# A decoder trunk's first mixer: q, k and v projected in plain fp32 while the first adaLN products stream, o, x and y from raw weights

## What is computed

```python
c_act = silu(c)
for layer in range(2):
    shift, scale, gate = split(c_act @ ada_w[layer, 0] + ada_b[layer, 0], 3)
    hn = rmsnorm(x, norm_g[layer, 0]) * (1 + scale) + shift
    y = rglru_mlstm_mixer(hn, ...) if layer == 0 else stick_breaking_mixer(hn, ...)
    x = x + gate * y
    shift, scale, gate = split(c_act @ ada_w[layer, 1] + ada_b[layer, 1], 3)
    hn = rmsnorm(x, norm_g[layer, 1]) * (1 + scale) + shift
    x = x + gate * ((silu(hn @ w1) * (hn @ w3)) @ w2)
return rmsnorm(x, final_g)

# mixer of layer 0
xa, ya, q, k, v, o, ig, fg = split(h @ w_in)        # 1024, 1024, 512, 512, 1024, 1024, 4, 4 columns
xa = conv4(xa); out_a = rglru(xa) * gelu(ya)
hb = mlstm_chunkwise(q, k, v, ig, fg)               # 4 heads, running sums of the gates
out_b = norm(hb) * sigmoid(o)
y = concat(out_a, out_b) @ w_out
# mixer of layer 1: q, k, v = h @ w_qkv; 16 heads of stick-breaking attention; o @ w_out
```

## Time and profile before

| | us |
|---|---|
| median of three runs | 2453.87 (2453.47 to 2454.26) |
| profiled execution | 2454.73 |
| its span, first to last instruction | 2453.0 |
| TensorE busy | 2266.0 (92%) |
| VectorE busy | 1887.5 (77%) |
| ScalarE busy | 1028.7 (42%) |
| first product of the output projection of layer 0 | at 406.03 |

### The profile page before, as it was taken

How to read it: one execution, slowest core, us unless ns; L and a number is a source line. 1 busy time by engine, 2 the same in 40 slices (tenths; PEclk the granted TensorE clock), 3 DMA queues, 4 the chain that set the end, 5 groups by cost and what they waited for, 6 DMA issues and landing times.

```text
span 2453.0 us, 36210 instructions
## 1 busy us (share of the span) xinstructions
PE 2266.0 (92%) x12638; PEld 1956.7 (80%) x12638; DVE 1887.5 (77%) x2347; ACT 1028.7 (42%) x1183; POOL 245.9 (10%) x209
## 2 busy tenths in 40 slices
PE   0289998989999999999989999998999999999998
PEld 0277887778888888888878888887888888888887
DVE  7888897988887888778896666678887566666667
ACT  1134456344433443344455455534443344433443
POOL 6100000510000000000240000033000000000014
PEclk9989998999999999999999999999999999999999
DMA  8798775867777776777756655665776555555554
GB/s 345 292 377 312 280 282 210 308 236 282 282 271 286 279 285 270 287 277 289 280 215 272 243 222 219 244 241 212 301 276 255 188 189 188 188 188 188 188 201 159
DMA packets 86186, 619.80 MB, mean 253 GB/s; under 512 B 10216, under 2 KB 10472, under 8 KB 10984
## 3 DMA queue, kind: packets, MB, share of 16 engines
q1 hardware_dynamic: 85248, 617.79, 65.7%
q10 hardware_dynamic: 872, 1.15, 0.1%
HBM read 616.80 MB, written 2.10 MB: 252 GB/s over the span
## 4 chain that ended last, share of the span: by engine, by line
PE 83%; DVE 10%; issue 3%; POOL 2%; ACT 1%; DMA 0%; DVEq 0%; POOLq 0%; ACTq 0%
PE ps L962 49%; PE ps L960 12%; PE ps L965 12%; PE ps L934 4%; DVE adaw L585 3%; DVE wlow L577 3%; PE ps L911 2%; POOL work L381 1%; POOL work L375 1%; PE ps L913 1%; DVE raw L585 1%; ACT whigh L415 1%; DVE work L703 1%; PE ps L1085 1%; DVE hn L709 0%
## 5 line engine op out<-in xcount | busy, mean ns | idle before, releaser
L415 ACT ACTIVATE whigh<-raw 128x1024 fp32r<-128x1024 f32 x784 | 828.0, 1060 | 1182.5 <-PE ps L962 1113.7
L577 DVE TENSOR_TENSOR wlow<-raw,whigh 128x1024 fp32r<-128x1024 f32 x784 | 974.3, 1261 | 391.3 <-ACT whigh L415 382.6
L962 PE MATMUL ps<-hn,whigh 128*128 128x512 f32 x3712 | 1174.6, 397 | 5.1 <-DVE wlow L577 5.1
L962 PE MATMUL ps<-mid,whigh 128*128 128x512 f32 x1856 | 588.0, 397 | 8.5 <-DVE wlow L577 8.5
L962 PEld LDWEIGHTS ps<-hn,whigh 128*128 128x128 f32 x3712 | 569.1, 189 | 7.2 <-issue 6.8
L960 PE MATMUL ps<-hn,wlow 128*128 128x256 f32 x1856 | 517.7, 279 | 0.0
L965 PE MATMUL ps<-hn,wlow 128*128 128x256 f32 x1856 | 515.9, 278 | 0.0
L960 PEld LDWEIGHTS ps<-hn,wlow 128*128 128x128 f32 x1856 | 349.5, 188 | 85.0
L965 PEld LDWEIGHTS ps<-hn,wlow 128*128 128x128 f32 x1856 | 350.3, 189 | 79.6
L585 DVE CUSTOM_DVE_ANT_0 adaw<-adaw,cact 128x2048 f32<-128x2048 f32 x176 | 407.1, 2316 | 5.8 <-DMA adaw<-ada_dram 5.6
L962 PEld LDWEIGHTS ps<-mid,whigh 128*128 128x128 f32 x1856 | 284.9, 189 | 12.2 <-DVE wlow L577 7.6
(11 more groups left out here) (197 smaller groups left out, 1243.6 us busy)
## 6 DMA issues: line engine op xcount, KB each, us to landing
raw<-wts_dram SPq DMA_DIRECT2D x392, 1024.0 KB, 4.8
adaw<-ada_dram SPq DMA_DIRECT2D x176, 1024.0 KB, 6.7
raw<-ada_dram SPq DMA_DIRECT2D x16, 1024.0 KB, 5.6
x<-xT_dram SPq DMA_DIRECT2D x1, 2048.0 KB, 13.9
out_dram<-x SPq DMA_DIRECT2D x4, 512.0 KB, 2.6
cact<-c_row_dram SPq DMA_DIRECT2D x1, 1024.0 KB, 5.1
work<-lru_w_dram ACTq DMA_DIRECT2D x1, 1024.0 KB, 6.6
mod<-ada_b_dram SPq DMA_DIRECT2D x1, 96.0 KB, 4.3
```

The costliest lines, as they stand in the source:

```text
L415: act.activation(whigh[:, (2 * s + h) % 4, :], raw[:, s, h * HALF:(h + 1) * HALF], ACT.Copy)\
L577: dve.tensor_tensor(wlow[:, half, :], raw[:, s, h * HALF:(h + 1) * HALF], whigh[:, half, :].bitcast(F32), ALU.subtract).then_inc(S["low_re ...
L962: ins = pe.matmul(ps[:, s, :], whigh[:, half, w], src[:, kk, :, :], start=kk == 0, stop=kk == kts - 1, skip_group_check=True)
```

## The change

There are 94 bodies and 16 start tiles; the bytes loaded are the same.

**Start.** GpSimd's sums of squares for the first norm are gone: x is loaded in four parts, ScalarE squares them, VectorE adds the four, TensorE sums over the partitions with a matrix of ones, and the root is taken for all tokens on all partitions (`rstd_full`). VectorE scales tile k in step k of the prologue, ScalarE adds the shift, and the activations are kept as plain fp32 (`hn_full`, in the place of `hn`'s first half). The weights of q, k and v come as 16 rows of 1 MB, one for each tile of the contraction, into slots 0 and 1 of `raw` and a part of `work` (`extra`). For each tile TensorE does eight products of 256 columns for q and k in banks 0 to 3 and four of 512 columns for v in banks 4 to 7 (`start_tile`), with plain fp32 operands, and all eight banks gather over the 16 tiles.

**o, x, y.** Six bodies (`FULL`) multiply the raw chunk with `hn_full`, 16 products of 256 columns, straight from `raw`; there is no split. SP reloads slot s when TensorE has multiplied it, and ScalarE alone evicts the bank. The units are now 6 a body (4 in the last), and 4 instead of 2 in the third body of out0. The steps of the recurrences stand inside the bodies, behind the slot that a dictionary names.

**Layer 1.** The steps scores, sums and values stand behind the second chunk of the following body; the last sums and values stand inside the first half body of out1, at tiles 6 and 12.

```diff
-    body(IN0, "qk", 0, 0, 16, 4, True)
...
-        body(IN0 + 8 + j, "y_branch", 0, j, 32 + j, 2, inner=("lru", j))
-        between("lru_out", j)
...
-    bodies(OUT0 + 2, DOWN - 2, "out0", 38, 2, i0=2)
+    body(IN0, "o", 0, 0, 16, 6, inner={0: ("gate_sums", None), 1: ("gate_rows", None), 3: ("head", 0)})
+    body(IN0 + 1, "o", 0, 1, 19, 6, inner={1: ("head", 1), 3: ("head", 2)})
+    body(IN0 + 2, "x_branch", 0, 0, 22, 6, inner={0: ("head", 3), 2: ("head", 4), 3: ("head_roots", None)})
+    body(IN0 + 3, "x_branch", 0, 1, 25, 6, inner={1: ("mlstm_out", None), 3: ("conv", None)})
+    body(IN0 + 4, "y_branch", 0, 0, 28, 6, inner={1: ("lru", 0), 3: ("lru_out", 0)})
+    body(IN0 + 5, "y_branch", 0, 1, 31, 4, inner={0: ("lru", 1), 3: ("lru_out", 1)})
+    body(OUT0, "out0", 0, 0, 33, 4, True)
+    body(OUT0 + 1, "out0", 0, 1, 35, 4)
+    body(OUT0 + 2, "out0", 0, 2, 37, 4)
+    body(OUT0 + 3, "out0", 0, 3, 39, 2)
...
     body(IN1, "q", 0, 0, 72, 2, True)
+    body(IN1 + 1, "k", 0, 0, 73, 2)
     with eng.Fori(0, 3) as g:
-        b = g * 3 + (IN1 + 1)
-        body(b, "k", 0, g, g * 3 + 73, 2)
-        between("scores", g)
-        body(b + 1, "vs", 0, g, g * 3 + 74, 2)
-        between("sums", g)
-        body(b + 2, "q", 0, g + 1, g * 3 + 75, 2)
-        between("values", g)
+        b = g * 3 + (IN1 + 2)
+        body(b, "vs", 0, g, g * 3 + 74, 2, inner={1: ("scores", g)})
+        body(b + 1, "q", 0, g + 1, g * 3 + 75, 2, inner={1: ("sums", g)})
+        body(b + 2, "k", 0, g + 1, g * 3 + 76, 2, inner={1: ("values", g)})
+    body(IN1 + 11, "vs", 0, 3, 83, 2, inner={1: ("scores", 3)})
+    between("last_sums", 3)
+    between("last_values", 3)
...
+                        if kind in FULL:
+                            sp.wait_ge(S["halves_multiplied"], n * 8 + 2 * s + 2 + CREDIT)
+                        else:
+                            sp.wait_ge(S["low_ready"], n * 8 + 2 * s + 2)
...
+                        if k >= 3:
+
+                            sp.wait_ge(S["start_done"], k - 2)
+                        place, loaded = start_place(k)
+                        sp.dma_start(place, wts[k, :, :]).then_inc(loaded, 16)
...
+                        while k >= RSTD_STEP and scaled_tiles <= k:
+                            m = scaled_tiles
+                            dve.wait_ge(S["slope_ready"], m + 1)
+                            dve.scalar_tensor_tensor(hn_full[:, m, :], x[:, m, :], slope[:, m:m + 1], rstd_full, ALU.mult, ALU.mult)\
+                               .then_inc(S["start_scaled"], 1)
+                            scaled_tiles += 1
...
+            def full_body(n, inner):
+
+                for s in range(CH):
+
+                    pe.wait_ge(S["chunks_evicted"], n * CH + s + 1)
+                    pe.wait_ge(weight_loaded[s], weight_count(n, s))
+                    for k in range(KT):
+                        ins = pe.matmul(ps[:, s, 0:T], raw[:, s, k * P:k * P + P], hn_full[:, k, :], start=k == 0, stop=k == KT - 1)
+                    ins.then_inc(S["halves_multiplied"], 2)
+                    if s in inner:
+                        between(*inner[s])
+
+            def start_tile(k):
+
+                pe.wait_ge(S["start_ready"], k + 1)
+                place, loaded = start_place(k)
+                pe.wait_ge(loaded, k // 3 * 16 + 16)
+                for t in range(8):
+                    ins = pe.matmul(ps[:, t // 2, t % 2 * T:t % 2 * T + T], place[:, t * P:t * P + P], hn_full[:, k, :],
+                                    start=k == 0 and t % 2 == 0, stop=k == KT - 1, skip_group_check=True)
...
+                for b in range(4):
+                    col = D // 2 + b % 2 * 512
+                    ins = pe.matmul(ps[:, 4 + b, :], hn_full[:, k, b // 2 * P:b // 2 * P + P], place[:, col:col + 512],
+                                    start=k == 0, stop=k == KT - 1)
```

More of the change, by code:

```diff
@@ L45 @@
 CREDIT = 4
-NORM_STEP = 7
-SPLIT_STEP = 12
 EARLY = 2 * KT
+RSTD_STEP = 1
+CONST_STEP = 3
 UP = [2 * n // CH for n in GROUPS]
@@ L180, in bass_trunk @@
         x = sb("x", [P, KT, T])
+        with nc.sbuf_tensor("hn_full", [P, KT, T], F32) as hn_full:
+            pass
         hn = sb("hn", [P, KT, 2, T], F32R)
@@ L228, in bass_trunk @@
         S = {n: sem(n) for n in names}
+        x_loaded = [sem(f"x_loaded{q}") for q in range(4)]
         QK, XC, X, Y = (work[:, i:i + 8, :] for i in (0, 8, 16, 24))
@@ L431, in body @@
                         act.activation(work[:, 2 + s // 2, :], work[:, s // 2, :], ACT.Silu).then_inc(S["silu_ready"], 1)
-                    if s == 1 and inner:
-                        between(*inner)
+                    if s in inner:
+                        between(*inner[s])
             def norm(i):
@@ L903, in fresh_half @@
                     elif kind == "out1":
+                        if kk == 6:
+                            between("sums", 3)
+                        elif kk == 12:
+                            between("values", 3)
                         pe.wait_ge(S["s_low"], kk // 2 + 1 + 2)
```

276 lines of the change are left out of this document (147 added, 129 removed).

## The result

The changed kernel takes **2439.14 us** (median; 2435.03 to 2440.77) against 2453.74 (2453.47 to 2454.26) for the kernel before, measured beside it: a ratio of 0.9938, 95% interval 0.9921 to 0.9955. It is faster, by 14.6 us; 36.5 were forecast (22.5 - 3 + 17), and the time lies 1 us above the range. The profiled execution took 2440.77 us, its span is 2439.1.

What follows compares the result with a forecast made beforehand. TensorE, busy 92% of the span, bounds the kernel by what it executes and where it waits. 2454.7 − 22.5 (out0's earlier start) + 3 (out0) − 17 (layer 1) = 2418 us; forecast 2410 to 2427 (52%), range 2400 to 2438.

Steps and rivals of the forecast that it cites:

- The start: Layer 0's q, k, v tiles: loads at 395 GB/s set the end, first o product at 146 us.
- the first rival: Start's loads run at only 345 GB/s, o starts at 165, total 2437 us; chance 12%.
- TensorE's work in o, x, y: Layer 0's o, x, y stage: chunks, gates, heads and output rows take TensorE 206 us without waits.
- The five waits: In o, x, y up to out0, TensorE waits for five late steps, 25.7 us together.
- the layout: Step timetable from o's start: unit loads issued behind TensorE's chunk, then reduced before the inner step, make five steps late.
- Four of them add 6: In o, x, y: half clock behind four of the five waits, some 1.7 us each, adds 6 us.
- out0: Layer 0's output projection: four units instead of two in its third body cost 3 us, bound 0 to 4.6.
- Layer 1: Second layer: scores moved behind the next body's second chunk save four times 4.3 us, −17 us.
- the four waits: TensorE's waits before layer 1's score products, 11.2 us in all, for the eviction of k's last chunk.
- late next would be the masks: Layer 1: GpSimd's masks would be the next late input; 0 to 1 us of wait at k-tile 12.
- gives nothing back: Rival on layer 1: steps inside bodies delay VectorE's splits by what the waits cost before; 2433 us, chance 13%.
- The slower rival: In o, x, y unit loads queue, landing times above 13 us, all five steps later; about 2460 us, chance 6%.

Runs made afterwards that it cites:

- the run without waits: Changed kernel with, in o, x, y, each chunk's two unit loads issued ahead of the weight reload on SyncE's queue: 2408.68 us.
- the runs with altered orders: Changed kernel with VectorE's inner step ahead of the units, 2410.59 us; with unit loads ahead of the weight reload on SyncE, 2408.68 us; with both, 2409.06 us.
- the run with the units laid out evenly: Changed kernel with 6 adaLN units instead of 4 in the second y body and 2 instead of 4 in out0's third body: 2439.55 us.
- the kernel with all four edits: Changed kernel with unit loads before weight reloads, lru(1) earlier, vs in banks 1 and 2, last sums ahead of out1, units 6 per fp32 body, then 4, 4, 2, 2: 2393.49 us.

## Why the prediction was wrong

**The start: right in its end, in part by luck.** O began at 145.5 (146 forecast) with the first tile at 30.39, and a tile takes 6.9 us as the sum had it. Twelve of the sixteen tiles ran at TensorE's pace (6.89 us apart) and not at the 8.0 of the forecast's loads. The last four are 7.45 us apart: there VectorE waits for each pair of units, and three loads of 1.05 MB in 7.45 us are the 422 GB/s that the DMA engines gave. In order of time:

```profile
109.08 3.62 PE L993 MATMUL ps<-hn_full,raw 128*128 128x256 f32 x16
...
123.62 3.72 PE L993 MATMUL ps<-hn_full,raw 128*128 128x256 f32 x16 [0.30 <-ACT hn_full L484]
```

```profile
117.26 2.29 DVE L609 CUSTOM_DVE_ANT_0 adaw<-adaw,cact 128x2048 f32<-128x2048 f32 x1 [1.69 <-DMA adaw<-ada_dram]
```

So the loads set the end, as forecast, but only by 1.9 us (at 6.89 a tile from 40.21 on it would have been 143.6), and by other terms: 53.6 MB at 422 GB/s are 127 us and not 136, and what was gained there went elsewhere. SP's wait for `start_done`, which was to cost nothing, held the loads until 40.41 (DMA share 0.25 from 38 to 41), since the first tile ran its eight products of 256 columns in 6.4 us instead of 3.5 and was done at 40.2, not 38; and between the last unit's data at 134.65 and the last tile at 138.52 lie that unit's 2.3 us and the last steps, 3.9 us where the sum had 1. The window from 60 to 120 (busy of PE, PEld, DVE, ACT, POOL, PEclk, share, GB/s):

```profile
60.00:120.00 60.00, 59.96 (x212) 40.00 (x211) 43.53 (x57) 4.06 (x8) 0.00 (x0) 1.00 1.01 422
```

422 GB/s at a share of 1.01 is above the 395 of the forecast and the 345 of the first rival, which is out. The rule that the Trainium skill gives in "DMA: Bandwidth & Descriptors", section "Specifications", some 358 GB/s for one core, does not agree with this row either. The falling clock that the Trainium skill tells of in "TensorE: Matmul & The Clock Gate", section "A second HAM failure mode: psum-queue depth-cycling", did not come: the granted clock is 1.00 in this window and to the end of the tiles, whose waits are 0.3 us.

**TensorE's work in o, x, y: right.** 206 forecast, 207.7 busy in the run without waits.

**The five waits: right in place and nearly in size.** Head 0 4.5 forecast and 3.94 measured, head 3 4.2 and 4.02, head roots 3.8 and 4.18, the first recurrence half 7.2 and 8.75, out0 6.0 and 8.26; 25.7 and 29.2 together. For the first four the mechanism of the layout, a unit's load issued only behind TensorE's own chunk and the step behind the unit, is what the runs with altered orders showed from two sides (the head roots' wait ends with ScalarE's last copy, not with VectorE's). The fifth, ahead of out0, stood behind lru 1 and the units as laid out, but with VectorE's queue full and not with late data, so neither order cured it. The forecast priced all five at 32 us, and so the first four at 25.7 (19.7 and 6 for the clock); the two orders gave 28.6 and 30.5 for these four.

**The clock: the first step that failed.** "Four of them add 6", at 1.7 us each, was read off a single window behind a wait of before, where TensorE went on with a dense row of projection products. Here 13 us went, about half of them behind head 3's wait alone (half clock from 241 to 254). These 7 us more, 3.5 more in the waits and 1.7 more work, less 0.5 at the start, make out0 start 11.8 us later than forecast. Why the clock stays low three times as long there as behind the head roots' wait (282 to 286), no run here settles. Behind the wait at 241 come small products of the heads, some on four rows, and projection products again only from 250.78, at 282 they come again from 283.71, and the clock came back only behind them in both; no run tried a dense row of products behind head 3's wait, so this rival stands untested. The long stretch is no accident of one execution: in the run with the units laid out evenly the clock is at 0.50 from 242 to 250 and at 0.55 up to 254.

**out0: nearly right.** +4.4 instead of +3, within its bound; some 3.8 of it are the third body's two units, as the experiment with 4, 4, 2, 2 shows.

**Layer 1: the second step that failed, and the larger single miss.** Forecast -17, measured -8.7: the sum took the four waits and the partly cold products behind them as gone with nothing in their place. They went, and "late next would be the masks" was wrong: no mask is waited for. Next in line were two things in the shadow of the removed waits, vs's group in bank 3, which needs the same eviction (four times 1.4 us), and the splits ahead of out1 (2.9 us), which sums and values had covered. The rival "gives nothing back" had VectorE's and ScalarE's queues delayed by the inner steps; that is half of its price, but not its mechanism. With both removed, in the kernel with all four edits, layer 1 gains 18.0 us, which is the forecast's 17 within what executions differ by.

The misses add up: 11.8 up to out0, 1.4 in out0, 8.3 in layer 1, 21.5 in all; the profiled execution lies 22.8 above 2418 (the median 21), and 1 of the rest is in the two FFNs, which the forecast took as unchanged.

**The slower rival** priced late unit loads at landing times above 13 us. The units' loads land after 6.9 us as the median and 10.2 at most, so it did not come in that form; the loads were late because they were issued late.

## What to carry to other kernels

Look at where a prefetch is issued, not only at how long it takes: behind a wait for products of TensorE that it has nothing to do with it comes late, and everything that stands behind its user in an in-order queue comes late too. Here turning over two lines in one queue was worth twice the whole change. When a wait is removed, list every other instruction that needs the same event, and everything that was done in its shadow; those are the new waits. And price a wait of TensorE by what it does to the clock behind it: in this stage 20 us of waits cost 33. Then look at each wait for its own cause: four of the five here were late data, the fifth a full queue, and an edit made for the one did nothing for the other.

## What the runs showed of the hardware that was not expected

- After a wait of about 4 us TensorE ran at or near a granted clock of 0.50 for between 4 us (282 to 286, window at 0.58) and 12 us (242 to 254, at 0.50), though it was busy all the time in both. In the kernel before, the clock fell to 0.59 over 303 to 307 with no wait ahead, right behind eight products on four rows. There the stretch behind out0's wait has 0.71 over 6 us, in the changed kernel 0.60 over 8 us; the same instructions follow.
- A lone core's loads kept 422 GB/s for 60 us (60 to 120) at a DMA share of 1.01, while VectorE and TensorE worked on.
